# A decode step of a hybrid S5 and latent-attention layer: cache pages turned in 32x32 blocks on another engine

## What is computed

```python
sc = (q_abs . c + q_pe . k_pe) * SOFTMAX_SCALE      # causal: -inf right of the diagonal
w  = softmax(sc);  o = (w . c) . w_uv
```

```python
c_past = c_pool[page_table]                          # (8, 2048, 512)
s_past = (q_abs . c_past + q_pe . kpe_past) * SOFTMAX_SCALE
w = softmax([s_past, s_new]);  o_lat = w . [c_past, c_new]
```

## Time and profile before

| | |
|---|---|
| median of 3 runs | 1160.72 us (1159.94 to 1162.0) |
| the profiled execution | 1159.42 us, of which 1157.7 from first to last instruction |
| TensorE busy | 1088.8 us, 94% |
| VectorE, ScalarE, GpSimd busy | 51%, 33%, 14% |
| mean granted TensorE clock | 0.984 of 2.4 GHz |
| attention stage | 717 to 942 us |
| HBM read and written | 141.5 MB and 24.9 MB |

### The profile page before, as it was taken

One profiled execution on the slowest core, in us unless ns is written; L12 is line 12 of the kernel. 1 busy time (PEld: TensorE's weight loads), 2 busy tenths in 40 slices (PEclk: granted clock), 3 DMA queues, 4 the chain that ended last, 5 costly groups with the idle time before them and its releaser, 6 DMA issues.

```text
span 1157.7 us, 25426 instructions
## 1 busy us (share of the span) xinstructions
PE 1088.8 (94%) x9906; PEld 1009.7 (87%) x9906; DVE 586.7 (51%) x1243; ACT 384.8 (33%) x761; POOL 164.8 (14%) x252
## 2 busy tenths in 40 slices
PE   3899999999999999998899999899999989999995
PEld 2899999999999999987799986677677659999995
DVE  4366454451688821395665355655555452332432
ACT  6321112112233312154542223444444442332433
POOL 3002310000310000103505401022233100000000
PEclk9899999999999999998999999999999999999998
DMA  9446743223344442236456755377777777223213
GB/s 280 101 139 117 161 120 93 71 69 92 115 122 124 120 134 84 73 97 224 131 156 194 236 183 177 121 219 228 226 225 232 207 232 258 77 78 103 72 36 148
DMA packets 200149, 169.99 MB, mean 147 GB/s; under 512 B 36139, under 2 KB 164630, under 8 KB 198230
## 3 DMA queue, kind: packets, MB, share of 16 engines
q1 hardware_dynamic: 177398, 120.51, 37.1%
q0 software_dynamic: 11168, 27.93, 8.4%
q10 hardware_dynamic: 11496, 20.36, 4.8%
HBM read 141.49 MB, written 24.91 MB: 144 GB/s over the span
## 4 chain that ended last, share of the span: by engine, by line
PE 84%; DVE 5%; DMA 4%; ACT 4%; issue 2%; ACTq 0%; SPq 0%; DVEq 0%; POOL 0%; POOLq 0%
PE gemm L1981 12%; PE gemm L1982 12%; PE gemm L1983 12%; PE gemm L2345 5%; PE gemm L2347 5%; PE gemm L2346 5%; PE misc L2257 5%; PE gemm L2297 3%; PE gemm L2276 3%; PE misc L2243 2%; PE misc L2057 2%; PE misc L2067 1%; PE misc L2008 1%; DMA w_raw<-w_glu 1%; DMA w_raw<-w_in 1%
## 5 line engine op out<-in xcount | busy, mean ns | idle before, releaser
L1981 PE MATMUL gemm<-xh,w_hi 128*128 128x260 f32 (+2 forms) x1056 | 302.3, 286 | 0.3 <-DVE w_lo L1274 0.3
L1982 PE MATMUL gemm<-xl,w_hi 128*128 128x260 f32 (+2 forms) x1056 | 300.7, 285 | 0.0
L1983 PE MATMUL gemm<-xh,w_lo 128*128 128x260 f32 (+2 forms) x1056 | 299.9, 284 | 0.0
L1274 DVE TENSOR_TENSOR w_lo<-w_raw,w_hi 128x2048 fp32r<-128x2048 f32 (+3 forms) x63 | 109.0, 1730 | 227.4 <-ACT w_hi L830 224.3
L830 ACT ACTIVATE w_hi<-w_raw 128x2048 fp32r<-128x2048 f32 (+3 forms) x63 | 90.7, 1439 | 336.5 <-PE gemm L1983 285.1
L1981 PEld LDWEIGHTS gemm<-xh,w_hi 128*128 128x128 f32 x1056 | 198.8, 188 | 1.2 <-DVE w_lo L1274 0.6
L1983 PEld LDWEIGHTS gemm<-xh,w_lo 128*128 128x128 f32 x1056 | 199.1, 189 | 0.0
L1982 PEld LDWEIGHTS gemm<-xl,w_hi 128*128 128x128 f32 x1056 | 198.8, 188 | 0.0
L2345 PE MATMUL gemm<-comb_hi,w_hi 128*128 128x260 f32 x512 | 147.0, 287 | 1.1 <-DVE comb_lo L1861 1.1
L2347 PE MATMUL gemm<-comb_hi,w_lo 128*128 128x260 f32 x512 | 144.7, 283 | 0.0
L2346 PE MATMUL gemm<-comb_lo,w_hi 128*128 128x260 f32 x512 | 144.7, 283 | 0.0
(11 more groups left out here) (369 smaller groups left out, 2073.9 us busy)
## 6 DMA issues: line engine op xcount, KB each, us to landing
w_raw<-w_in SPq DMA_DIRECT2D x35, 1024.0 KB, 6.5
ckv<-cache_ckv POOLq DMA_DIRECT2D x72, 256.0 KB, 3.5
w_raw<-w_out SPq DMA_DIRECT2D x16, 1024.0 KB, 5.9
ckv<-cache_ckv SPq DMA_DIRECT2D x56, 256.0 KB, 3.0
z_d<-ev ACTq DMA_DIRECT2D x16, 260.0 KB, 2.1
w_raw<-w_glu SPq DMA_DIRECT2D x8, 512.0 KB, 4.5
yt<-x_prompt SPq DMA_DIRECT2D x4, 1024.0 KB
o_y_p<-yt SPq DMA_DIRECT2D x4, 1024.0 KB
```

The costliest lines, as they stand in the source:

```text
L1274: dve.tensor_tensor(w_lo[:, slot, 0:width], w_raw[:, slot, 0:width], w_hi[:, slot, 0:width].bitcast(F32), ALU.subtract).then_inc(w_lo_read ...
L1981: pe.matmul(acc, a, xa, start=k == 0, stop=False)
L1982: pe.matmul(acc, a, xb, start=False, stop=False)
L1983: last = pe.matmul(acc, b, xa, start=False, stop=k == k_tiles - 1)
```

## The change

Pages are turned on VectorE, by instructions that transpose each 32x32 block in place: four of 128x512 and one of 128x256 a group, from `ckv` and `kpe` into `ct` and `kt` in SBUF. Block `(a, r)` of a page then holds 32 latent values of the 32 positions of quarter `a`. To contract these, the query becomes block-diagonal: `qx` has 32 columns, `8 * a + h`, whose rows of quarter `a` hold the 32 latent values of head `h` and the others zero. A page group takes 16 + 2 k-steps times four pages, each of 32 weight columns and 32 moving ones, in place of 4 + 1 times four of 8 and 128. `SC` has two halves, for samples in turn. `rep` holds the query values repeated over the quarters, made ahead of the loop by 16 products with pieces of the identity and 8 small loads; `build_query` (ScalarE, 8 copies) makes `qx` for each sample. The sample's maximum now goes over the quarters (two small transposes), the weights are turned by VectorE and spread by 16 small products (`spread_page_weights`).

The causal mask is added by a product of the identity with `causal` in fp32r within `scores`; `ident` and `causal` are therefore copied by ScalarE from `raw`. `normalise` no longer touches `prob`: it builds a diagonal of reciprocals, `diag`, and `turn_weights` multiplies with it in fp32, where it transposed. All four groups of a sample are weighed in the first tile of the next, and every later page group is loaded in halves: pages 0 and 1 by SyncE, 2 and 3 by GpSimd.

```diff
         def freed_at(i):
-            return 4 * (i // 4) + 4 + (i % 4 if i // 4 < N_SAMPLE - 2 else i % 4 // 2)
+            return 4 * (i // 4) + 4
...
-            for i in range(RING + 1, N_GROUPS_OF_PAGES, 2):
-                load_group(pool, i)
+            for i in range(RING, N_GROUPS_OF_PAGES):
+                load_pages(pool, i, (1,), 0)
...
-                tt(diag, diag, causal[:], ALU.add).then_inc(max_step, 1)
...
-                p = prob[:, m % 2, 0:keys_of(m)]
-                dve.tensor_scalar(p, p, r, None, ALU.mult).then_inc(prob_ready, 1)
+                if m >= 2:
+                    dve.wait_ge(pt_ready, rounds(m - 1))
+                dve.tensor_scalar(diag[:, m % 2], ident[:], r, None, ALU.mult).then_inc(prob_ready, 1)
...
+            def turn_pages(n, first, last):
+                if first == 0:
+                    for by_sync, count in enumerate(loaded_counts(n)):
+                        if count:
+                            dve.wait_ge(page_loaded[by_sync][n % RING], count)
+                    if n >= 2:
+                        dve.wait_ge(sc_ready, n - 1)
+                for x in range(first, last):
+                    dve.transpose(out=ct[:, n % 2, x, :], in_=ckv[n % RING][:, x, :])
+            def turn_rotary(n):
+                dve.transpose(out=kt[:, n % 2].rearrange("p x e -> p (x e)"), in_=kpe[n % RING][:].rearrange("p x e -> p (x e)")
+                              ).then_inc(page_turned, 1)
...
+                if own is not None:
+                    pe.matmul(own, ident[:].bitcast(F32R), causal[:].bitcast(F32R), start=False, stop=False)
...
-                    last = pe.transpose(TP[:, j * P:(j + 1) * P], p[:, j * P:(j + 1) * P], ident[:])
+                    last = pe.matmul(TP[:, j * P:(j + 1) * P], p[:, j * P:(j + 1) * P], weight, start=True, stop=True)
...
             def page_scores(n):
                 s, g = divmod(n, 4)
+                pe.wait_ge(page_turned, n + 1)
+                if g == 0:
+                    pe.wait_ge(query_built, s + 1)
+                    if s >= 2:
+                        pe.wait_ge(sexp_done, s - 1)
+                c0 = (s % 2) * P + g * 32
+                for r in range(16):
                     for j in range(4):
-                        pe.matmul(SC[32 * j:32 * j + N_HEADS, cols], qa[:, r, s, :], ct[:, n % 2, r, j, :], start=r == 0, stop=False)
+                        pe.matmul(SC[32 * j:32 * j + 32, c0:c0 + 32], qx[:, s % 2, r, :], ct[:, n % 2, j, r * 32:(r + 1) * 32], start=r == 0, stop=False)
...
             for n in range(N_TILES):
-                turn_rope(n)
-                turn_page(n, 0)
                 if n + 1 < N_TILES:
                     scores(n + 1)
                 if n % 4 == 0 and n:
                     turn_last_weights(n - 1)
-                turn_page(n, 1)
-                turn_page(n, 2)
+                    weigh_values(n // 4 - 1)
+                    spread_page_weights(n // 4 - 1)
+                turn_weights(n)
                 if n % 4 == 0 and n:
-                    turn_page_weights(n // 4 - 1)
-                    weigh_values(n // 4 - 1)
-                turn_weights(n)
-                turn_page(n, 3)
-                for i in range(N_GROUPS_OF_PAGES - 4):
-                    if freed_at(i) == n:
-                        weigh_pages(i // 4, i % 4)
+                    for c in range(4):
+                        weigh_pages(n // 4 - 1, c)
```

More of the change, by code:

```diff
@@ L408, in build @@
         SPLIT_AT = {26: (0,), 30: (1, 2, 3), 31: (4, 5, 6)}
[L410 to L424, removed]
         def rounds(m):
@@ L438, in freed_at, with loaded_counts, load_pages @@
         def freed_at(i):
-            return 4 * (i // 4) + 4 + (i % 4 if i // 4 < N_SAMPLE - 2 else i % 4 // 2)
[L442 to L452, removed]
+            return 4 * (i // 4) + 4
+        BY_SYNC = 3
+        def loaded_counts(i):
+            whole = (0, 128) if i % RING == BY_SYNC else (128, 0)
+            return [w + 64 * (i // RING) for w in whole]
+        def load_pages(eng, i, halves, by_sync):
+            pages = [eng.value_load(ptab[0:1, 4 * i + j:4 * i + j + 1], min_val=0, max_val=d["cache_ckv"].shape[1] - 1)
+                     for half in halves for j in (2 * half, 2 * half + 1)]
             if i >= RING:
                 eng.wait_ge(opv_done, pages_freed(i - RING))
[L455 to L458, removed]
+            s = i % RING
+            for at_j, page in enumerate(pages):
+                half, j = halves[at_j // 2], 2 * halves[at_j // 2] + at_j % 2
+                eng.dma_start(ckv[s][:, j, :], d["cache_ckv"][0, ds(page, 1)].rearrange("a k r -> (a k) r")).then_inc(page_loaded[by_sync][s], 16)
+                eng.dma_start(kpe[s][:, j, :], d["cache_kpe"][0, ds(page, 1)].rearrange("a k r -> (a k) r")).then_inc(page_loaded[by_sync][s], 16)
         MX, NMS, SMS = 0, 8, 16
@@ L2205, in _ @@
                     last.then_inc(c_t_ready, 1)
+                    if t == 0:
+                        pe.wait_ge(rope_done, 5)
+                        for q in range(4):
+                            for a in range(4):
+                                last = pe.matmul(misc[2 + q // 2][32 * a:32 * a + 32, (q % 2) * 256:(q % 2 + 1) * 256].rearrange("p (k m) -> p k m", k=4),
+                                                 ident[:, 32 * q:32 * q + 32], qa[:, 0:4].rearrange("p k b h -> p k (b h)"), start=True, stop=True)
+                        last.then_inc(qa_ready, 1)
             pe.wait_ge(rope_done, 5)
@@ L2281, in turn_page_weights @@
-            def turn_page_weights(s):
-                n = 4 * s + 4
-                pe.wait_ge(sexp_done, s + 1)
-                bank = await_bank(n, "weights")
-                for c in range(4):
-                    last = pe.transpose(bank[:, c * P:(c + 1) * P], pr[:, c * P:(c + 1) * P], ident[:])
-                last.then_inc(unit_ready, 1)
+                pe.wait_ge(page_turned, n + 1)
+                if g == 0:
+                    pe.wait_ge(query_built, s + 1)
+                    if s >= 2:
+                        pe.wait_ge(sexp_done, s - 1)
@@ new lines, in page_scores @@
+                c0 = (s % 2) * P + g * 32
+                for r in range(16):
+                    for j in range(4):
+                        pe.matmul(SC[32 * j:32 * j + 32, c0:c0 + 32], qx[:, s % 2, r, :], ct[:, n % 2, j, r * 32:(r + 1) * 32], start=r == 0, stop=False)
+                for e in range(2):
+                    for j in range(4):
+                        last = pe.matmul(SC[32 * j:32 * j + 32, c0:c0 + 32], qxr[:, s % 2, e, :], kt[:, n % 2, j, e * 32:(e + 1) * 32],
+                                         start=False, stop=e == 1)
@@ new lines, in page_scores, with spread_page_weights @@
+                last.then_inc(sc_ready, 1)
+            def spread_page_weights(s):
+                pe.wait_ge(sc_step, 7 * s + 7)
+                if s:
+                    pe.wait_ge(weights_copied, s)
+                by_quarter = prt[:].rearrange("p (g a h) -> p a g h", g=4, a=4)
+                for j in range(4):
+                    for a in range(4):
+                        last = pe.matmul(T_BANK[0][32 * a:32 * a + 32, j * 32:(j + 1) * 32].rearrange("p (g h) -> p g h", g=4),
+                                         ident[:, 32 * j:32 * j + 32], by_quarter[:, a], start=True, stop=True)
+                last.then_inc(weights_ready, 1)
```

279 lines of the change are left out of this document (147 added, 132 removed).

## The result

The changed kernel takes 1197.2 us (median of 4 runs, 1192.8 to 1202.9) against 1160.9 before: a ratio of 1.032 (95% interval 1.029 to 1.035), 36 us slower. The forecast was 1165, its range 1140 to 1190. The profiled execution took 1201.0 us, 1199.2 from first to last instruction, against 1157.7.

What follows compares the result with a forecast made beforehand. TensorE was taken as the bound, 26.2 of 26.9 us a round. +3.3 - 1.0 - 1.0 + 0.5 + 0.5 = +2.3, plus 1.7 for a half-clock stretch: 1160.7 + 4 = 1165 us, own range 1155 to 1173, overall 1140 to 1190.

Steps and rivals of the forecast that it cites:

- The bound and the unit costs: In the stage TensorE bounds, 26.2 of 26.9 us; page scores cost 1.45 us a tile, a 128x512 turn 0.62.
- transposes two a cycle: VectorE's page turns run two elements a cycle, saving 2.2 us a round: 1148 us, chance 0.18.
- small products: Each page-score record takes its own slot on TensorE, 2.6 us more per tile: 1248 us, chance 0.07.
- two cycles an element: VectorE's page turns take two cycles an element, 6.4 us more a round: 1215 us, chance 0.08.
- The low bound: TensorE page scores with four column groups at once: 36 rounds of four at 31 ns, 1.1 us a tile.
- The walk: From one maximum to the next over four tiles, TensorE and VectorE waiting for each other: 26.95 us against 27.1 measured.
- the ring: Scores wait behind page scores, these for VectorE's turns, these behind a maximum needing scores; TensorE's gain is given back as waiting.
- The failed step: Round time in the stage: busy sums of 20.8 us TensorE and 20.4 VectorE allow 21; mutual waiting makes it 26.95.
- rival two: A half-clock stretch in every round, in tiles 4k+1 or 4k+3: 1176 us, 1190 with two a round; chance 0.20.
- Ahead of the stage: Before the page tiles, query-spreading products and query build end the first page scores 3.3 us later.
- First round: The stage's loose first round, TensorE busy 21.6 us, takes back 1.0 us of the later start.
- The end: After the rounds: longer maximum and weight turn ahead of the last weighing 0.5 us, splits of finished heads 0.5.

Runs made afterwards that it cites:

- experiment 13: Changed kernel with 44 page-score records a tile as partial sums, the adding products ahead of the next scores at each sample's end: 1177.6 us.
- 7: Changed kernel with 44 page-score records a tile as partial sums, and VectorE's last two turns and rotary turn ahead of the next maximum: 1143.7 us.
- 9: Changed kernel with half the latent steps left out and 64 unread small records issued behind the next tile's scores instead: 1184.6 us.
- 10: Changed kernel with all 144 page-score records a tile, split into two bursts, the first two pages ahead of the weight turn: 1193.4 us.
- 1: Changed kernel with only TensorE's order altered, page scores of tile n behind the scores of tile n+2: 1204.1 us.
- experiment 5: Changed kernel with 44 page-score records a tile as partial sums, added up behind the next tile's scores: 1190.8 us.
- 8: Changed kernel with 44 page-score records a tile as partial sums, plus ten unread 256-column products ahead of the wait for turned pages: 1191.4 us.
- 11: Changed kernel with 44 page-score records a tile, VectorE's turns ahead of the next maximum, and weighings behind the same tile's page scores: 1140.3 us.
- experiment 12: Changed kernel without the page loads of groups 7 and up, later tiles working on pages already there: 1177.9 us.
- 4: Changed kernel with every other latent step of the page scores left out, 80 records a tile and not 144: 1154.9 us.
- experiment 2: Changed kernel with eight more unread 512-column products a tile ahead of the wait for turned pages: 1215.6 us.
- 3: Changed kernel with 64 more unread small fp32 products, 128 records, a tile ahead of the wait for turned pages: 1311.4 us.

## Why the prediction was wrong, point by point

**The bound and the unit costs: right.** Two 128x512 turns take 1.29 us and one 0.69, the rotary one 0.40, as taken. The page scores of tile 13 and the scores behind them (TensorE):

```profile
834.55 1.26 PE L2312 MATMUL gemm<-ct,qx 128*32 128x32 f32 x126 [1.79 <-DVE kt L1755]
...
835.91 0.39 PE L2201 MATMUL gemm<-hh 128*128 128x264 f32 x1
```

835.91 - 834.55 = 1.36 us for 144 records, taken 1.45. So the rivals "transposes two a cycle", "small products" and "two cycles an element" are out. The low bound had 27 ns and some 4 for loading weights for each four records; measured are 38 for the two together, and no run shows the 4 by itself. The Trainium skill's start-to-start floor ("TensorE: Matmul & The Clock Gate", "Wait — 56ns, not 53.3ns?") would give 3.6 us; the trace disagrees for products in four column groups, 9 ns a record. The Trainium skill's one element per cycle and lane ("Vector Engine (DVE) Microarchitecture Reference", "3.8 The reshape front-end and per-opcode configuration") fits the trace: 512 columns take 0.61 us from start to start, at the middle value of 0.62 that was taken and far from both ends, 0.43 and 1.15.

**The walk: right, and within 1 us.** Forecast 5.50, 5.27, 6.48, 9.70; shortest steps measured 5.34, 5.11, 6.51, 9.07, in all 26.0 for 26.95. The idle times stand where they were said to: TensorE's page scores wait for `kt` (25.6 us in 17 times from 750 to 930), VectorE's maxima for L2207. And the ring is what eats TensorE's savings: experiment 13 repeats it at 26.1 us with nothing else in the way, and 7 is at 23.5 once it is opened.

**The failed step: that a round is the longer of the walk and the busy sums.** The prediction counted the records (104 a tile more) only as time on the array. It had no term for bringing them: one packet of 16.4 KB for 126 to 128 records, at best one every 3.3 to 3.9 us in the kernels where they come back to back. A round issues 4250 / 6 = 708 records, 5.6 packets, so the undisturbed walk of 26.0 us leaves 4.6 us for each on average. Yet about once a round TensorE runs dry for 1.2 to 3.8 us. Why it does at that mean rate is open: 9 and 10 spread the records over the tile and kept the stops.

That the packets end the stops, their times show. A packet starts at 845.24 us and takes 0.98 us (this is the row of the queue from 845.2 to 845.3 us), so it lands at 846.21; the stop in the page scores of tile 15 ends at 847.77, 1.56 us later.

```profile
q8 instruction: 1, 0.02, 60.9%
```

All seven stops in the six rounds end 1.3 to 1.7 us after a packet has landed, though one lands only every 5.6 us. So do all 90 stops of more than 1 us that end by nothing in the six rounds of the changed kernel and of experiments 1 to 13: 1.2 to 1.7 us. The six kernels with 59 to 61 packets (the one before, and 5, 7, 8, 11 and 13) have no such stop there.

With 100 records a tile fewer the same walk lost 3.5 us in six rounds (experiment 13), not 33.7; so nearly all that the rounds lost came with the records. The stops themselves make 17.9 of the 33.7 us. The rest, some 16 us, is put down to the half clock; no experiment shows it alone. The rows of before that could have warned are its 59 packets and, in the stage, 16 in 180 us, one in 11 us.

**The half clock, rival two: the price right, the number of stretches far too small.** The price was right: where a stretch falls on the step from tile 4k+2 to 4k+3 in experiment 5, it takes 6.78 us and not 5.20, 1.6 for the 1.7 taken. The sum had 1.7 us for one stretch more; in the six rounds the clock falls nine times, for 53 us together. The cause was sought in TensorE's waits for turned pages. They do not bring a fall in every round: in experiment 12 the same walk with the same waits (1.8 and 2.0 us) runs nearly two rounds without a stop, and the clock stays at 2.4 GHz until a stop of 3.6 us ends that stretch:

```profile
864.70:915.80 51.10, 37.59 (x1291) 27.55 (x1280) 37.53 (x96) 17.58 (x58) 0.00 (x0) 1.00 0.26 72
```

In the changed kernel four of the nine falls from tile 4 to 28 begin in a stop or right behind one (815.6, 846.4, 931.7 and 938.5 us). Ahead of four others the longest idle time of TensorE is a wait for a turned page, 1.8 to 2.0 us, as the rival had it. Experiments 4 and 5 have nine falls each with no stop near one (clock 0.90 and 0.91). So both causes are there, and how many of the falls the stops brought is not shown. How the 5.6 us a round divide is not exact: 3.0 for stops by their own gaps, or 4.1 by experiment 2, which holds the clock up but adds instructions. Both leave the clock the smaller part.

**Ahead of the stage: forecast +3.3, measured +7.0**, and 5.1 of these stand already at the turn of the last head's weights, ahead of any changed product (678.25 us against 673.16), 2.3 of them at that of the first. Other kernels with the same beginning reached tile 0 between 716.3 and 721.5 us, so most of this is scatter of one execution; the changed part is 1.9. **First round: forecast -1.0, measured +3.2**: half clock from 730.3 to 744.0 us. **The end: forecast +1.0, measured +2.8:** half clock for 10 us between 959.0 and 976.1 us, where the kernel before has none, and no stop of more than 1 us.

**Sum.** Forecast for the profiled execution +4.0, measured +41.6. The difference is 29.5 in the six rounds (+28.6 for -0.9), 4.2 in the first, 3.7 ahead of the stage and 1.8 at the end, less the 1.7 put in for a half-clock stretch.

## What to carry to other kernels

Count instructions as a resource of their own: see on the page how many packets the instruction queue takes in the stage. In this stage 16 in 180 us (one in 11 us) made no stop, 25 (one in 7.2) one of 1.2 us in six rounds, 32 (one in 5.6) seven. Many small products that use the array well can lose to fewer than a third as many wider ones with a copy and an extra sum behind them. And when two engines wait for each other in a ring, less work or a faster supply shows only in part until the ring is opened: try both edits together before dropping either.

## What was not expected of the hardware

Instructions reach TensorE in packets of 16.4 KB on a queue of their own while the kernel runs. The Trainium skill ("Trainium Architecture — The Big Picture", "The software stack") gives an instruction 64 bytes; by that I estimate 256 to a packet, and 126 records a packet agrees with two a record, its weight load and its product. Packets back to back start no closer than 3.3 us (experiments 3 and 9), and with the page traffic taken away 3.4; the stops get shorter without it, but do not go. TensorE goes on 1.2 to 1.7 us after a packet has landed. What starts a fetch, and how far ahead of TensorE it reaches, no run here shows. Also not expected: 144 fp32 records of 32 by 32 in 1.36 us, and a clock that stays at 2.4 GHz through 140 us in which TensorE idles 21%, in pieces of up to 1.6 us.
